# Combining the expert results of a two-layer block: accumulating transfers from GpSimd instead of loads and TensorE sums

## The chip, the cores and the metric

The kernel runs on one core of one Trainium2 chip. The metric is the device time of one execution in microseconds (us), the median of several runs. A core has TensorE (PE in the rows; PEld is its weight load), VectorE (DVE), ScalarE (ACT), GpSimd (POOL) and SyncE (SP), and 16 DMA engines that move data between the device memory and the on-chip memory. Each engine runs its own instructions in program order and waits on semaphores for the others.

## The reference

All arithmetic is float32. Two layers over 1040 rows (16 meta rows and 1024 tokens) of 1024 columns: layer 0 mixes by a state-space recurrence and differential attention, layer 1 by a gated linear recurrence (RG-LRU). After each mixer stands a layer norm and then a mixture of experts, each token going to two of 32 experts:

```
for i in range(DEPTH):
    mix = mixer_i(h)
    h = _layer_norm(ALPHA * h + mix, ln1_g, ln1_b)
    h = _layer_norm(ALPHA * h + _hier_moe(h, ...), ln2_g, ln2_b)
return h[:, N_META:]

def _layer_norm(z, g, b):
    mu = mean(z); var = mean((z - mu)**2)
    return (z - mu) * rsqrt(var + LN_EPS) * g + b
```

`_hier_moe` gives for a token the sum over its two experts of gate times expert output; ALPHA is the fourth root of 4, about 1.41. The change is in how the second of these two norms gets its input in each layer.

## The kernel before

**Stages.** The program is a chain of phases; a phase ends when all engines have met (`end_phase`). In order: layer 0's mixer, layer 0's experts and combining (`experts_and_combine`, layer 0), layer 1's mixer (`rglru_and_project`), layer 1's experts and combining. The rows are cut in 9 tiles (`TILES`): tile 0 with 16 meta rows, tiles 1 to 8 with 128 rows each. Layer 1 doesn't compute tile 0 in its combining, so it has 8.

**Experts.** SP loads the experts' weights in 96 units of 2 MB into a ring of 10 slots at the bottom of the on-chip memory (`l_w_ring`); each load waits until TensorE has read the unit that was in its slot. TensorE multiplies, ScalarE and VectorE scale each result by its gate (`K.gates`, `K.big_gate`), and GpSimd scatters the scaled rows with indirect DMAs to a buffer in device memory, `K.y_dram` (`expert_rows` in the rows). It has 2 x 1040 rows: first results, then second results. The last work items are two experts with a full block each (`big(4)`, `big(5)`) and a pair of small ones. `OverBlocks` handles blocks that the main plan has no room for.

**Combining** (`class Combining`, line 2146). When GpSimd has seen its last scatter land, it counts up `rows_done` (line 1839). SP waits for that and then loads, for each tile, two tiles of expert rows (`l_y`, line 2177) and the old rows out of `K.h1_dram` into `K.H` (line 2178), four tiles ahead. The gain and bias of the norm are loaded behind the second tile (`Norm.load`, line 1027). TensorE adds the two expert tiles by products with the identity into PSUM (`y_sum`, line 2234); VectorE makes ALPHA times old row plus that sum (line 2215, two instructions a tile; the first tile is done wholly by VectorE in lines 2210 and 2211). Then the norm of the tile: VectorE takes statistics (lines 1034 to 1036), subtracts the mean and multiplies by the gain (1041), ScalarE takes the root (1056), VectorE the reciprocal (1045), ScalarE scales (1060), GpSimd adds the bias (1068). For the last tile VectorE does the last two in one instruction (1050), after a wait for GpSimd's bias additions of all tiles before it. SP stores the tile (2184), to `K.h2_dram` in layer 0 and to the output in layer 1.

**Layer 0 alone.** TensorE turns each finished tile (`turn`, line 2243) and ScalarE copies it to `K.hT` (line 2260), which the next phase multiplies. ScalarE's program is one row of instructions: `norm.scalar(j)`, then the copies of tile j - 2. Between its stores SP also loads the first two blocks of RG-LRU weights (lines 2289 to 2292) and eight parameter vectors, by channel, with one element to a descriptor (lines 2297 and 2299). At its end SP waits for all stores (line 2199), and the phase ends.

**The next phase.** TensorE starts with the products of line 2343. VectorE first works out a table of parameters (lines 2437 to 2455) that it needs from line 2411 on.

## Time and profile before

| | us |
|---|---|
| median of 3 runs | 2360.14 (2353.16 to 2363.47) |
| the profiled execution, its own time | 2359.76 |
| its span in the trace | 2357.8 |
| layer 0, from the last scatter's issue to the first product of the next phase | 1180.3 to 1251.7 |
| layer 1, from the last scatter's issue to the last instruction | 2298.8 to 2354.8 |

All positions are us from the start of the span. A timeline line has start, duration, engine, line of the kernel, operation, output<-inputs, and in square brackets how long the engine sat idle before it and what ended that. SPq and POOLq are the queues of instructions that issue DMAs.

### The profile page before, as it was taken

The page shows a single profiled execution, that of the slowest core. Times are in us where ns is not written, and L with a number is a line of the kernel's source. Part 1 is how long each engine was busy: PE and PEld are TensorE (multiplying, and loading weights), DVE is VectorE, ACT ScalarE, POOL GpSimd, SP SyncE. Part 2 cuts the span into 40 slices and gives each one's busy share as a digit, 9 for nine tenths or more (in the row PEclk, how much of TensorE's full clock was granted, in tenths as well). Part 3 has the DMA queues.
Part 4 walks back from the last instruction along what each step waited for, and adds up shares of the span by engine and source line. Part 5 has one row for each costly group of instructions (what it writes and reads, how often), then busy time and mean ns, then how long its engine had stood idle before and what let it go on. Part 6 is the DMA issues. An engine that isn't in the chain of part 4 may idle for free. (4 is left out here: it accounts for less than half of the span.)

```text
span 2357.8 us, 33523 instructions
## 1 busy us (share of the span) xinstructions
PE 2188.0 (93%) x13475; PEld 1240.7 (53%) x13475; DVE 766.4 (33%) x1608; ACT 486.0 (21%) x904; POOL 308.5 (13%) x263
## 2 busy tenths in 40 slices
PE   7999999999689999999968999999967999999994
PEld 5787656655454555455434555555544455545541
DVE  7652236652611111111173444442261111111116
ACT  2222236611001001000023444431100100100001
POOL 7253000011011111111030000001101111111102
PEclk9999999999789999999988999999978999999998
DMA  4110002112399999899885111111239999989987
GB/s 159 38 37 1 21 1 72 32 40 70 141 401 418 420 419 418 343 398 410 368 298 165 40 32 29 40 39 37 71 135 395 414 421 418 420 350 393 413 367 306
DMA packets 148199, 529.81 MB, mean 225 GB/s; under 512 B 43874, under 2 KB 66946, under 8 KB 131664
## 3 DMA queue, kind: packets, MB, share of 16 engines
q1 hardware_dynamic: 134608, 493.84, 53.2%
q0 software_dynamic: 13312, 33.84, 3.7%
q8 instruction: 107, 1.75, 0.3%
q14 instruction: 44, 0.36, 0.0%
q10 hardware_dynamic: 128, 0.02, 0.0%
HBM read 499.99 MB, written 39.98 MB: 229 GB/s over the span
## 5 line engine op out<-in xcount | busy, mean ns | idle before, releaser
L1884 PE MATMUL l_main_pgu<-l_w_ring,l_ex_xT 128*64 128x256 f32 (+1 forms) x4992 | 473.5, 385 | 11.8 <-DMA l_w_ring<-in_l_moe_w_gate 8.5
L1884 PEld LDWEIGHTS l_main_pgu<-l_w_ring,l_ex_xT 128*64 128x64 f32 (+1 forms) x4992 | 285.6, 129 | 188.9 <-issue 41.5
L1930 PE MATMUL l_main_py<-l_w_ring,l_ex_hT 128*64 128x512 f32 (+1 forms) x1248 | 231.9, 595 | 1.9 <-DVE l_ex_hT L2002 1.9
L1881 PE MATMUL l_main_pgu<-l_w_ring,l_ex_xT 128*128 128x512 f32 x384 | 170.1, 597 | 1.7 <-DMA l_w_ring<-in_l_moe_w_gate 1.6
L1998 DVE TENSOR_TENSOR l_ex_hid<-l_ex_sil,l_main_pgu 128x256 f32<-128x256 f32 (+1 forms) x76 | 35.2, 463 | 376.0 <-PE l_main_pgu L1884 278.8
L2343 PE MATMUL lru_pr<-h2T,lru_wz 128*128 128x352 f32 (+1 forms) x480 | 144.4, 462 | 10.3 <-ACTq L2398 10.3
L2002 DVE COPY l_ex_hT<-l_main_ph 128x256 f32<-128x256 f32 (+1 forms) x76 | 35.4, 466 | 363.7 <-PE l_main_ph L1905 363.7
L2361 PE MATMUL lru_pg<-h2T,lru_wz 128*128 128x512 f32 x320 | 148.7, 592 | 0.0
L1930 PEld LDWEIGHTS l_main_py<-l_w_ring,l_ex_hT 128*64 128x64 f32 (+1 forms) x1248 | 69.2, 127 | 132.1 <-issue 124.8
L1976 ACT ACTIVATE l_ex_sil<-l_main_pgu 128x256 f32<-128x256 f32 (+1 forms) x76 | 31.7, 417 | 464.9 <-PE l_main_pgu L1884 372.5
L2343 PEld LDWEIGHTS lru_pr<-h2T,lru_wz 128*128 128x128 f32 x480 | 92.6, 193 | 63.1 <-ACTq L2398 10.7
L1881 PEld LDWEIGHTS l_main_pgu<-l_w_ring,l_ex_xT 128*128 128x128 f32 x384 | 71.2, 190 | 90.9 <-issue 87.0
L1822 POOL DMA_INDIRECT expert_rows<-l_ex_yb,half_row x64 | 64.2, 1003 | 414.4 <-issue 218.2
L308 PE MATMUL s_pa<-hT,w_in 128*128 128x260 f32 x512 | 114.7, 383 | 0.0
L1068 POOL TENSOR_TENSOR H<-H,l_ln_bias 128x1024 f32<-128x1024 f32 (+1 forms) x30 | 70.5, 2349 | 334.7 <-ACT H L1060 334.7
L1160 PE MATMUL lru_pr<-w_out,y1T 128*128 128x512 f32 x240 | 107.0, 602 | 0.0
L308 PEld LDWEIGHTS s_pa<-hT,w_in 128*128 128x128 f32 x512 | 96.9, 190 | 16.3 <-issue 1.7
L2361 PEld LDWEIGHTS lru_pg<-h2T,lru_wz 128*128 128x128 f32 x320 | 60.8, 190 | 57.1 <-issue 43.0
L1960 ACT COPY l_ex_xT<-l_main_px 128x512 f32<-128x512 f32 (+1 forms) x52 | 27.0, 520 | 295.0 <-PE l_main_px L1853 295.0
L2234 PE MATMUL l_main_pgu<-l_y,ident 128*128 128x512 f32 x88 | 45.2, 652 | 40.4 <-DMA H<-h_rows 40.1
L1041 DVE SCALAR_TENSOR_TENSOR H<-H,l_ln_mean_var,l_ln_gain 128x1024 f32<-128x1024 f32 (+1 forms) x34 | 50.5, 1485 | 95.5 <-PE lru_pg L1185 46.4
L1808 POOL DMA_INDIRECT l_ex_xb<-h_rows,x_idx x36 | 37.4, 1038 | 332.4 <-PE l_main_px L1853 212.3
...
## 6 DMA issues: line engine op xcount, KB each, us to landing
...
```

Of the source, the lines that this page charges most:

```text
L308: last = pe.matmul(pa[n % 2][:, 0:STEPS], w[:, k, P * (f % HEADS):P * (f % HEADS) + P], hT[:, k, j, :], start=k == 0, stop=k == KD - 1)
L1041: dve.scalar_tensor_tensor(out=z, in0=z, scalar=self.mv[0:m, 0:1], in1=self.gain[0:m, :], op0=ALU.subtract, op1=ALU.mult).then_inc(self.ga ...
L1068: pool.tensor_tensor(z, z, self.bias[0:m, :], ALU.add).then_inc(self.h_ready, 1)
L1160: last = pe.matmul(po[j % 2][h][0:m, :], self.slices[k][:, t0:t0 + m], self.w_out[:, k, 512 * h:512 * h + 512], start=k == 0, stop=k == ns ...
L1808: pool.indirect_dma_start(xb[xn % 2][0:m, :], None, K.h1_dram, bass.IndirectOffsetOnAxis(ap=index, axis=0), bounds_check=T - 1, oob_is_err ...
L1822: pool.indirect_dma_start(y_halves, bass.IndirectOffsetOnAxis(ap=K.half_row[:, it.column:it.column + 1], axis=0), yb[i % 2][:, 0:512], Non ...
L1881: last = pe.matmul(out[:], x[:, k, :], w[0][:, k, :], start=k == 0, stop=k == KD - 1)
L1884: last = pe.matmul(out[HALF * h + o:HALF * h + o + m, 0:256], x[:, k, it.at + o:it.at + o + m], w[n][:, k, 256 * h:256 * h + 256], start=k ...
L1930: last = pe.matmul(py[b][HALF * h + o:HALF * h + o + m, :], hT[:, c % 2, HALF * (c // 2) + o:HALF * (c // 2) + o + m], ws[n][:, c, 512 * h ...
L2234: last = pe.matmul(self.ps[j % 2][h][0:m, :], K.ident[0:m, 0:m], self.y[k][j % B][0:m, 512 * h:512 * h + 512], start=k == 0, stop=k == 1)
L2343: last = pe.matmul(pr[j][:, 0:c], wz[par][:, k, 0, :], K.hT[:, k, o:o + c], start=k == 0, stop=k == KD - 1)
L2361: last = pe.matmul(pgt[j][:, 0:c], wz[par][:, k, 1, :], K.hT[:, k, N_META + o:N_META + o + c], start=k == 0, stop=k == KD - 1)
```

## The change

It does five things.

- **Gates.** `K.gates` is scaled by 1/ALPHA, so that old row plus the two results is z/ALPHA; the norm gets LN_EPS/ALPHA² instead of LN_EPS and gives the same rows. The scaling takes the place of a copy.
- **Old rows ahead.** The tiles of `K.h1_dram` are loaded into a new buffer `z`, which lies in the ring's slots 6 to 8, as soon as the last units in these have been read, while the last experts are still being computed. Gain and bias follow when slot 9 has been read.
- **Accumulating transfers.** GpSimd adds both expert results onto `z` with DMAs that accumulate (`accum_op=ALU.add`), first results of tile j, and four tiles behind second results, each of which waits until the first one of its tile has landed. TensorE's sums and VectorE's additions are gone; VectorE's norm starts when both have landed and writes `K.H` from `z`.
- **RG-LRU loads.** The weights of the first two blocks are loaded when TensorE is done with the ring. The parameters are loaded as rows ahead of that, turned by one TensorE instruction at the start of the next phase, and copied by VectorE.
- **Stores.** Layer 0's stores are no longer waited for in their own phase, but in the next one ahead of `project.sync`.

The core of the diff:

```
+ROW_UNITS, NORM_UNIT = (6, 7, 8), 9
+LEAD = 4
@@ in route
-        do(dve.tensor_copy(K.gates[:], ptab[:, 1, :]))
+        do(ts(K.gates[:], ptab[:, 1, :], 1.0 / ALPHA, None, ALU.mult))
@@ experts_and_combine, SP, behind the last weight load
+            for unit in range(3 * NE):
+                if unit + UNITS >= 3 * NE and unit % UNITS in ROW_UNITS:
+                    unit_used(unit)
+            combine.load_rows(sp)
...
+            combine.load_norm(sp)
             sp.wait_ge(ya_ready, acts[N])
@@ GpSimd
             over.gpsimd(pool, blocks)
-            pool.sem_inc(rows_done, 1)
             combine.gpsimd(pool)
@@ TensorE
             over.tensor(pe)
+            pe.sem_inc(ring_free, 1)
             combine.tensor(pe)
@@ class Combining
+    def load_rows(self, sp):
+        for i in range(self.first, NT):
+            t0, m = TILES[i]
+            sp.dma_start(self.z[0:m, i, :], self.K.h1_dram[t0:t0 + m, :]).then_inc(self.rows_loaded, 16)
+
+    def load_norm(self, sp):
+        self.norm.load(sp, self.A[self.L + "_ln2_g"], self.A[self.L + "_ln2_b"])
+        if not self.last_layer:
+            self.K.lru.load_parameters(sp, self.free)
...
     def sync(self, sp):
+        if not self.last_layer:
+            sp.wait_ge(self.ring_free, 1)
+            K.lru.load_weights(sp, 0, 0)
+            K.lru.load_weights(sp, 1, 1)
+        for j in range(self.n):
             t0, m = TILES[self.first + j]
             sp.wait_ge(norm.h_ready, j + 1)
             sp.dma_start(out, K.H[0:m, self.first + j, :]).then_inc(self.stored, 16)
-        sp.wait_ge(self.stored, 16 * self.n)
+        if self.last_layer:
+            sp.wait_ge(self.stored, 16 * self.n)
 
     def gpsimd(self, pool):
+        def add(k, j):
+            t0, m = TILES[self.first + j]
+            if k == 1:
+                pool.wait_ge(self.added[j], 16)
+            pool.dma_start(self.z[0:m, self.first + j, :], K.y_dram[k * T + t0:k * T + t0 + m, :], accum_op=ALU.add).then_inc(self.added[j], 16)
+
+        pool.wait_ge(self.rows_loaded, 16 * n)
+        for j in range(n + LEAD):
+            if j < n:
+                add(0, j)
+            if j >= LEAD:
+                add(1, j - LEAD)
         for i in range(self.first, NT - 1):
             self.norm.gpsimd(pool, i)
 
+    def vector(self, dve):
+        do = Order(dve, self.order)
+        for j in range(self.n):
+            i = self.first + j
+            dve.wait_ge(self.added[j], 32)
+            self.norm.vector(dve, do, i, rows=self.z[0:TILES[i][1], i, :])
@@ rglru_and_project
         def _(sp):
+            sp.wait_ge(prm_turned, 1)
             load_w_out(sp, K, 1)
...
             sp.wait_ge(gate_ready, NG * NB)
+            sp.wait_ge(*K.h2_stored)
@@ TensorE
+            pe.wait_ge(R.loaded, 5 * 16)
+            pe.transpose(pa[0][:, 0:8 * NB], R.prm_rows[0:8 * NB, :], K.ident[0:8 * NB, 0:8 * NB]).then_inc(prm_turned, 1)
@@ VectorE
-            dve.wait_ge(R.loaded, 8 * 16)
+            dve.wait_ge(prm_turned, 1)
+            do(dve.tensor_copy(prm[:, 0:8, :].rearrange("p a n -> p (a n)"), pa[0][:, 0:8 * NB]))
```

`Combining.scalar` is not touched, nor is the body of `turn`.

Where GpSimd's program of layer 0 comes out of `OverBlocks` (the branches) and into the combining, before:

```order
L2046 UNCONDITIONAL_BRANCH
L2050 UNCONDITIONAL_BRANCH
L1068 TENSOR_TENSOR H<-H,l_ln_bias 16x1024
L1068 TENSOR_TENSOR H<-H,l_ln_bias 128x1024 x7
L1754 UNCONDITIONAL_BRANCH
```

and with the change (line 2218 is the accumulating DMA of `add`, 1069 the bias addition):

```order
L2061 UNCONDITIONAL_BRANCH
L2065 UNCONDITIONAL_BRANCH
L2218 DMA l_z<-expert_rows 16x1024
L2218 DMA l_z<-expert_rows 128x1024 x4
L2218 DMA l_z<-expert_rows 16x1024
L2218 DMA l_z<-expert_rows 128x1024 x12
L1069 TENSOR_TENSOR H<-H,l_ln_bias 16x1024
L1069 TENSOR_TENSOR H<-H,l_ln_bias 128x1024 x7
L1757 UNCONDITIONAL_BRANCH
```

Eighteen DMA issues now stand ahead of the first bias addition; before there was none.

SP's queue at the end of layer 0's combining, before, from the last tile's loads on:

```order
L2177 DMA l_y_5768<-expert_rows 128x1024
L2177 DMA l_y_5772<-expert_rows 128x1024
L2178 DMA H<-h_rows 128x1024
L2184 DMA h_rows<-H 128x1024
L2289 DMA lru_wz_5686<-in_l_w_in 128x8x128
L2290 DMA lru_wz_5686<-in_l_w_in 128x8x128
L2291 DMA lru_wax_5684<-in_l_lru_w_a 128x128
L2292 DMA lru_wax_5684<-in_l_lru_w_x 128x128
L2297 DMA lru_prm<-in_l_conv_w 128x10x1 x4
```

and with the change the same stretch, from the second block's weights to the end of the phase:

```order
L2289 DMA lru_wz_5687<-in_l_w_in 128x8x128
L2290 DMA lru_wz_5687<-in_l_w_in 128x8x128
L2291 DMA lru_wax_5685<-in_l_lru_w_a 128x128
L2292 DMA lru_wax_5685<-in_l_lru_w_x 128x128
L2207 DMA h_rows<-H 16x1024
L2207 DMA h_rows<-H 128x1024 x8
L1757 UNCONDITIONAL_BRANCH
```

Nothing but the waits for finished tiles now stands between SP's nine stores; before, both blocks of weights and the parameters stood between the fifth and the sixth.

ScalarE's program in layer 0's combining with the change (1057 the root, 1061 the scaling, 2259 the copies of a turned tile); its order is that of before:

```order
L1057 ACTIVATE l_ln_dev<-l_ln_var_eps 16x1
L1061 ACTIVATE H<-H,l_ln_rec_dev 16x1024
L1057 ACTIVATE l_ln_dev<-l_ln_var_eps 128x1
L1061 ACTIVATE H<-H,l_ln_rec_dev 128x1024
L1057 ACTIVATE l_ln_dev<-l_ln_var_eps 128x1
L1061 ACTIVATE H<-H,l_ln_rec_dev 128x1024
L2259 COPY h2T<-l_main_px 128x4x16 x2
L1057 ACTIVATE l_ln_dev<-l_ln_var_eps 128x1
L1061 ACTIVATE H<-H,l_ln_rec_dev 128x1024
```

Nothing moved here: the copies of tile 0 stand behind the scaling of tile 2 and ahead of the root of tile 3, as before.

## Rows read from the trace of the kernel before

**Rows 1.** Page, part 1: busy time, share of the span and instructions.

```profile
PE 2188.0 (93%) x13475; PEld 1240.7 (53%) x13475; DVE 766.4 (33%) x1608; ACT 486.0 (21%) x904; POOL 308.5 (13%) x263
```

**Rows 2.** Windows: length, engines' busy time (instructions), TensorE clock, DMA share, GB/s.

```profile
core 0: us, PE busy (x) PEld busy (x) DVE busy (x) ACT busy (x) POOL busy (x), PEclk, DMA share, GB/s
1130.00:1170.00 40.00, 39.03 (x221) 18.38 (x220) 4.35 (x7) 2.73 (x5) 1.95 (x2) 1.00 0.99 413
1170.00:1184.00 14.00, 7.57 (x43) 2.55 (x41) 1.83 (x3) 1.97 (x2) 1.96 (x2) 0.94 0.22 84
...
1190.00:1200.00 10.00, 5.84 (x8) 2.38 (x8) 4.44 (x8) 1.35 (x2) 0.23 (x1) 0.53 1.02 385
1200.00:1240.00 40.00, 34.23 (x124) 18.29 (x124) 37.97 (x64) 16.71 (x31) 18.60 (x8) 0.96 0.96 311
1240.00:1252.00 12.00, 1.70 (x8) 1.30 (x7) 0.37 (x4) 1.60 (x3) 0.00 (x0) 0.50 0.80 272
...
2291.00:2302.00 11.00, 5.09 (x37) 1.41 (x35) 1.83 (x3) 0.17 (x1) 1.97 (x2) 0.99 0.16 62
```

**Rows 3.** Timeline, layer 0: end of the experts, start of the combining.

```profile
1151.01 0.69 DVE L1998 TENSOR_TENSOR l_ex_hid<-l_ex_sil,l_main_pgu 128x512 f32<-128x512 f32 x1 [6.64 <-PE l_main_pgu L1881]
...
1180.29 0.98 POOL L1822 DMA_INDIRECT expert_rows<-l_ex_yb,half_row  x1 [3.87 <-DVE l_ex_yb L2010]
...
1184.49 1.37 SPq L2177 DMA_DIRECT2D l_y<-expert_rows  x2
...
1188.26 1.21 DVE L2210 SCALAR_TENSOR_TENSOR H<-H,l_y 16x1024 f32<-16x1024 f32 x1 [8.92 <-DMA H<-h_rows]
...
1196.71 1.27 DVE L1041 SCALAR_TENSOR_TENSOR H<-H,l_ln_mean_var,l_ln_gain 16x1024 f32<-16x1024 f32 x1 [4.20 <-DMA l_ln_bias<-in_l_ln_b]
```

**Rows 4.** Timeline, layer 0, VectorE and GpSimd: one tile of the steady part.

```profile
1213.76 1.28 DVE L2215 SCALAR_TENSOR_TENSOR H<-H,l_main_pgu 128x512 f32<-128x512 f32 x2
...
1215.12 2.37 POOL L1068 TENSOR_TENSOR H<-H,l_ln_bias 128x1024 f32<-128x1024 f32 x1 [2.48 <-ACT H L1060]
...
1216.72 1.85 DVE L1041 SCALAR_TENSOR_TENSOR H<-H,l_ln_mean_var,l_ln_gain 128x1024 f32<-128x1024 f32 x1
...
1218.60 0.69 DVE L2215 SCALAR_TENSOR_TENSOR H<-H,l_main_pgu 128x512 f32<-128x512 f32 x1
```

**Rows 5.** Timeline: end of layer 0's combining, start of the next phase.

```profile
1238.06 1.28 DVE L1050 SCALAR_TENSOR_TENSOR H<-H,l_ln_rec_dev,l_ln_bias 128x1024 f32<-128x1024 f32 x1
...
1239.40 1.97 PE L2243 MATMUL l_main_px<-ident,H 128*128 128x128 f32 x8 [0.57 <-DVE H L1050]
...
1241.17 3.48 SPq L2184 DMA_DIRECT2D h_rows<-H  x4
1241.40 1.07 ACT L2260 COPY h2T<-l_main_px 128x512 f32<-128x512 f32 x2 [1.47 <-PE l_main_px L2243]
...
1251.66 17.04 PE L2343 MATMUL lru_pr<-h2T,lru_wz 128*128 128x352 f32 x48 [10.30 <-ACTq L2398]
...
1269.21 0.82 DVE L2411 TENSOR_SCALAR lru_xc<-lru_rec,lru_pc 128x1040 f32<-128x1040 f32 x1 [9.81 <-ACT lru_rec L2378]
```

**Rows 6.** Timeline: a phase end with its stores not waited for, into layer 1's experts.

```profile
1735.33 0.26 DVE L1288 SCALAR_TENSOR_TENSOR logits<-lru_pa,l_ln_rec_dev,l_shift 128x36 f32<-128x36 f32 x1
...
1736.88 0.19 DVE L1611 TENSOR_REDUCE l_rt_cm<-logits 128x9 f32<-128x36 f32 x1 [1.30 <-PEq L2494]
```

**Rows 7.** Timeline, layer 1: last scatter, first load, last instruction.

```profile
2298.81 0.99 POOL L1822 DMA_INDIRECT expert_rows<-l_ex_yb,half_row  x1 [3.87 <-DVE l_ex_yb L2010]
2302.36 1.62 SPq L2177 DMA_DIRECT2D l_y<-expert_rows  x2
...
2353.49 1.28 DVE L1050 SCALAR_TENSOR_TENSOR H<-H,l_ln_rec_dev,l_ln_bias 128x1024 f32<-128x1024 f32 x1
```

**Rows 8.** Page, part 6: DMA issues, KB each, median us from issue to landing.

```profile
expert_rows<-l_ex_yb,half_row POOLq DMA_INDIRECT x64, 8.2
```

**Rows 9.** Line 1822 in 1150 to 1184: landing of layer 0's last scatter.

```profile
DMA to landing us min/median/max: 3.6/3.6/3.6
```

147 lines of the change are left out of this document (55 added, 92 removed).

## The prediction, made before the changed kernel ran

> **What bounds the kernel now.** I read the page first, then windows around the two places where the change works, then their timelines. TensorE is busy for 2188 of 2358 us [rows 1], and in the last 40 us of layer 0's experts for 39.0 of 40 [rows 2]: there the time is TensorE's, and nothing in the change touches its products. The combining is another matter. From 1200 to 1240 VectorE is busy for 37.97 of 40 us, TensorE for 34.2 (it adds expert rows there, which costs nothing while VectorE is later) and the DMA engines for 0.96 of the window at 311 GB/s [rows 2]. So VectorE sets the pace in that window, with the DMA engines close behind it: one tile every 4.84 us (line 2215 starts at 1213.76 and again at 1218.60) [rows 4].
>
> Two stretches are idle around it. The first tile's additions start at 1188.26, and VectorE then waits 4.20 us more for the norm's bias [rows 3]. At the end, ScalarE's last copy is done at 1241.40 + 1.07 = 1242.5, but SP issues the last four stores from 1241.17 to 1244.65, the phase waits for them to land, and the next phase's products start at 1251.66, 9.2 us after the copy [rows 5]. In layer 1 the combining starts at 2302.36 and VectorE's last instruction ends at 2353.49 + 1.28 = 2354.8 [rows 7].
>
> **Part 1: the end of layer 0's phase. Gain, 7.5 us.** The stores are waited for only in the next phase, ahead of work that is hundreds of us away. Another phase end in this trace has no such wait: last instruction ends at 1735.6, next phase's first starts at 1736.88, 1.3 us [rows 6]. So 9.2 shrinks to 1.3, less some 0.4 for the turn of the parameters, which now stands ahead of TensorE's products (one of eight products in a turn of 1.97 us takes 0.25) [rows 5]. VectorE's copy and parameter table are covered: it idles 9.81 us before line 2411 [rows 5]. If that cover were gone, a late parameter would cost its own lateness. The bounds are 6 and 8 us.
>
> **Part 2: old rows ahead. Cost: a later start of the adds, 3 us in layer 0, 2 in layer 1.** SP can load them when the up product of `big(5)` is read, just before 1151 [rows 3]; the weights in SP's queue before them keep the DMA engines full to about 1171 (share 0.99 up to 1170, then 0.22 over the next 14 us) [rows 2]. Nine tiles are 4.26 MB, 10.3 us at 413 GB/s; gain and bias 1.05 MB, 2.5 us; two scatters 1.9 us. That is 14.7 us behind 1171: 1185.7. It hides beside the last products, but the last scatter, issued at 1180.3, now travels in traffic. It took 3.6 us in silence [rows 9], the median over all is 8.2 [rows 8]; I take 3 of the 4.6 us between them, so GpSimd starts adding at 1184.3 + 3 = 1187.3. On top of that SP sends 2.36 MB of RG-LRU weights (5.7 us) from about 1180 on: the DMA engines are through with all that at 1191.4. In layer 1, with no RG-LRU loads, the weights end near 2291 (share 0.16 after it) [rows 2], and I put the start at 2302.1 + 2 = 2304.1.
>
> **Part 3: the price of an accumulating tile, u.** No row shows one, and the sum hangs on it. A plain tile of 0.524 MB takes 1.27 us at 413 GB/s and 1.36 at 385 [rows 2]: the lower bound, since the add can't move less. An add reads the expert rows and the old row and writes the sum: three passes where a plain load has two, 1.5 times, 1.9 to 2.0 us, if reads and writes cost alike; twice, 2.5 to 2.7 us, if the read side binds. I take the middle, **u = 2.3 us**, an estimate. For the issue on GpSimd the nearest row is the indirect DMA's 0.98 us [rows 3]; with some 0.3 for waits and registers, 1.3.
>
> The Trainium skill ("Collectives: The Full Stack", The bandwidth ceiling) says that a reducing transfer runs at half the rate of a copy because it needs two source reads, and gives a measured ratio of 1.93. By it u would be 2.45 to 2.6, a rival below; no row here shows it.
>
> **Part 4: layer 0's adds and norms.** GpSimd issues all 18 adds before its first bias addition. The last add waits for the first add of tile 8, which stands behind 11.1 tiles' worth of adds in the queue (a1 to a8, b1 to b3 and the small tile 0; a are first results, b second). The last issue is then at 1191.4 + 2.7 (landing and one issue) + 11.1u = 1194.1 + 25.5 = 1219.6. That matters for VectorE too, through ScalarE: ahead of the root of tile 3 stand the copies of tile 0, these wait for TensorE's turn, and this for GpSimd's bias addition of tile 0. So the norm stops at tile 3 until the adds are issued, although tiles 1 to 3 may have landed long before.
>
> From there: bias addition 2.4, turn 2.0, copy 1.1, root and reciprocal 0.3, 5.8 in all [rows 4, 5]. Then five more tiles on VectorE. Without the two line 2215 instructions (1.28, and gaps) a tile takes 4.84 - 1.32 = 3.52 [rows 4], so 17.6; and the last instruction 1.3: 24.7. The turn and copies at the end add 3.1, as before (1239.34 to 1242.5) [rows 5]. The copy ends at 1219.6 + 24.7 + 3.1 = 1247.4, 4.9 later than before. With part 1, layer 0 gains 7.5 - 4.9 = **2.6 us**. It also loses the 4.20 us bias wait and TensorE's adds, but both lie ahead of the stop and give nothing.
>
> **Part 5: layer 1.** No turns here, so ScalarE isn't held. The queue is a0 to a4, b0, a5, b1, a6, b2, a7, b3, b4 to b7. b3 lands at the start + 3.6 + 12u; from there tiles come faster (2.3 each) than VectorE takes them (3.52), and five tiles and the last instruction take 17.6 + 1.4. The end is 2304.1 + 22.6 + 27.6 = 2354.3, **0.5 us** sooner than 2354.8. GpSimd's bias additions don't bind: last issue at the start + 5 + 11u = 30.3, seven additions of 2.37 make 46.9, below 50.2. What follows the last instruction (one store) is as before.
>
> **The sum.** 2359.76 - 2.6 - 0.5 = 2356.7; the profiled run is 0.4 under the median, so no shift: **2357 us**. Each us on u costs 11.1 + 12 = 23.1 us over both layers. What a measurement of this kernel can tell from no change is about 0.5%, 11.8 us: u below 1.9 is faster by more, u above 2.9 slower. The gates' edit is an instruction for an instruction. The removed TensorE sums take the clock down earlier (it is 0.50 in the quiet windows [rows 2]), which I have paid for with 2.0 us a turn; before, the next phase started at 0.50 too.
>
> **Rivals.**
>
> *The adds run at the plain rate.* Then u = 1.3 and GpSimd's issue binds: 18 x 1.3 + 1 gives the last issue at 1187.3 + 24.4 = 1211.7, the copy at 1239.5, 3 sooner, 10.5 with part 1. Layer 1: b0 is the sixth issue and lands 11.4 after the start, eight tiles 28.2, last 1.4: 2345.1, 9.7 sooner. Sum 20: **2340 us**. For it: indirect transfers land in 3.6 us in silence, so the path itself is quick. Against it: an add moves half as much again. 0.2.
>
> *The read side binds,* so that an add takes about twice a plain tile, u = 2.55: 0.25 x 23.1 = 6 us more, **2363 us**, still within 0.5%. For it: in 1200 to 1240, with loads and stores mixed, the DMA engines were at 0.96 while moving 311 GB/s, less than with loads alone [rows 2]. 0.2. (This is what the rule of the Trainium skill, "Collectives: The Full Stack", The bandwidth ceiling, would make of it.)
>
> *Slower: an add goes through its passes one after another.* If reading old row, reading expert row and writing don't overlap within the DMA engines, u is about three plain tiles, 3.8, and the sum is 2356.7 + 1.5 x 23.1 = **2391 us**. Its place is the stretch up to the last issue in layer 0 and up to b3 in layer 1, and it decides from u = 2.9, or from an issue of 1.8 us on GpSimd if that binds instead (18 x 1.8 = 32 = 11.1 x 2.9). For it: nothing in this trace moves data so. [...] 0.22.
>
> *The forecast* without its neighbours: u between 1.55 and 2.9, 0.38, of which 0.13 lie under 1.9.
>
> **How the numbers follow.** Faster by over 0.5%: 0.2 + 0.13 = 0.33. Slower: 0.22. The rest, 0.45, is the forecast's main part and the second rival. The range takes in the plain rate at its end, 2340, and on the other side u = 3.2, 2357 + 0.9 x 23.1 = 2378. The unknown start (3 us in layer 0, 2 in layer 1, each may be 0 to 5) lies inside it.
>
> **What the profile after would show.** Accumulating DMAs on GpSimd's queue, GB/s in their window about 228 (0.524 MB in 2.3 us); VectorE idle in layer 0 from tile 2 to the end of the adds with ScalarE's wait for a turn behind it, then 3.5 us a tile; the next phase's products less than 2 us after the last copy; SP's row loads ending near 1182. Wrong would be the sum if the window of adds shows 390 GB/s or 130, if GpSimd's issues take well over 1.3 us, or if the last scatter lands much later than 1187.

## The result, and the profile after

The changed kernel takes **2381.07 us** (median of 6 runs, 2377.34 to 2383.67). The kernel before, run beside it, takes 2358.94 (2353.16 to 2363.47). The ratio is 1.010, 95% interval 1.0087 to 1.0112: slower by over 0.5%, and 3 us above the upper end of the range. The forecast was 2357.

The page of the changed kernel, busy time and the adds' row of the DMA issues (KB each, median us from issue to landing):

```profile
PE 2134.7 (90%) x13356; PEld 1220.8 (51%) x13356; DVE 757.9 (32%) x1575; ACT 486.3 (20%) x904; POOL 338.3 (14%) x297
...
l_z<-expert_rows POOLq DMA_DIRECT2D x32, 512.0 KB, 16.6
```

Against [rows 1], TensorE lost 53 us of work, VectorE 8.5, and GpSimd got 30 more, nearly all of it the issuing of 34 adds. No busy time says why the kernel is slower. Apart from the scaling of the gates and the loads that are sent ahead, all that changed lies behind the last scatter of each layer, so I measure everything from its issue:

| from the issue of the last scatter, us | before | after |
|---|---|---|
| layer 0: first load or add issued | 4.2 | 7.7 |
| layer 0: VectorE's last instruction ends | 59.1 | 77.0 |
| layer 0: next phase's products start | 71.4 | 83.2 |
| layer 1: first load or add issued | 3.6 | 8.6 |
| layer 1: VectorE's last instruction ends | 56.0 | 69.3 |

That is +11.8 in layer 0 and +13.4 in layer 1. The stretch from layer 0's next phase to layer 1's last scatter is 1047.15 us in both kernels. The span ends 4.3 us after VectorE's last instruction instead of 3.0, and this execution of the changed kernel came to layer 0's last scatter 3.5 us earlier (1176.81 against 1180.29). I don't count that as a gain: in the six runs built on the changed kernel or holding all that it loads ahead (the second, third, fifth, sixth, seventh and eighth below), the same scatter is issued anywhere from 1172.96 to 1182.77. Together 23.0, the difference of the two spans (2380.8 and 2357.8).

Timeline of the changed kernel, layer 0, GpSimd: last scatter, first and last adds, first bias additions:

```profile
1176.81 0.98 POOL L1837 DMA_INDIRECT expert_rows<-l_ex_yb,half_row  x1 [4.18 <-DVE l_ex_yb L2025]
1184.49 6.27 POOL L2218 DMA_DIRECT2D l_z<-expert_rows  x7 [6.69 <-issue]
...
1216.62 0.87 POOL L2218 DMA_DIRECT2D l_z<-expert_rows  x1 [4.71 <-DMA l_z<-expert_rows]
1222.16 0.87 POOL L2218 DMA_DIRECT2D l_z<-expert_rows  x1 [4.68 <-DMA l_z<-expert_rows]
1222.72 9.27 POOL L1069 TENSOR_TENSOR H<-H,l_ln_bias 16x1024 f32<-16x1024 f32 x4
```

The first add is 7.7 us behind the scatter (the first line answers to the scatter in [rows 3]). The last issues come one per 5.54 us, and each waits for the landing of an earlier add; an issue is paced by two adds, so an add takes 2.77. The bias additions start only behind the last issue, as forecast. The same stretches in windows, columns as in [rows 2]:

```profile
core 0: us, PE busy (x) PEld busy (x) DVE busy (x) ACT busy (x) POOL busy (x), PEclk, DMA share, GB/s
1188.00:1200.00 12.00, 0.00 (x0) 0.00 (x0) 0.00 (x0) 0.00 (x0) 6.72 (x9) 0.50 1.08 235
1200.00:1222.00 22.00, 0.00 (x0) 0.00 (x0) 11.38 (x23) 4.05 (x6) 4.79 (x6) 0.50 1.07 214
2334.00:2350.00 16.00, 0.00 (x0) 0.00 (x0) 9.63 (x20) 4.05 (x6) 4.85 (x5) 0.50 1.06 210
```

The DMA engines are full (1.06 to 1.08) while they move 210 to 235 GB/s; with plain loads and stores they moved 311 at 0.96 [rows 2]. Then the stop, and the tiles behind it, VectorE and GpSimd, layer 0:

```profile
1220.89 1.28 DVE L1042 SCALAR_TENSOR_TENSOR H<-l_z,l_ln_mean_var,l_ln_gain 128x1024 f32<-128x1024 f32 x1
...
1226.64 0.16 DVE L1046 RECIPROCAL l_ln_rec_dev<-l_ln_dev 128x1 f32<-128x1 f32 x1 [4.46 <-ACT l_ln_dev L1057]
1226.72 1.28 DVE L1035 BATCH_NORM_STATS2 l_ln_stats<-l_z 128x6 f32<-128x512 f32 x2
...
1228.35 4.73 DVE L1042 SCALAR_TENSOR_TENSOR H<-l_z,l_ln_mean_var,l_ln_gain 128x1024 f32<-128x1024 f32 x1
...
1234.47 2.34 POOL L1069 TENSOR_TENSOR H<-H,l_ln_bias 128x1024 f32<-128x1024 f32 x1 [2.48 <-ACT H L1061]
...
1234.75 3.15 DVE L1042 SCALAR_TENSOR_TENSOR H<-l_z,l_ln_mean_var,l_ln_gain 128x1024 f32<-128x1024 f32 x1
1237.82 0.15 DVE L1046 RECIPROCAL l_ln_rec_dev<-l_ln_dev 128x1 f32<-128x1 f32 x1
...
1239.29 2.34 POOL L1069 TENSOR_TENSOR H<-H,l_ln_bias 128x1024 f32<-128x1024 f32 x1 [2.47 <-ACT H L1061]
```

VectorE's reciprocal of tile 3 waits 4.46 us for ScalarE's root: the stop is there, at the tile that was named. But the tiles behind it take 1239.29 - 1234.47 = **4.82 us**, not 3.52. VectorE's subtract-and-multiply (line 1042, line 1041 before) takes 3.15 us; it took 1.85 in [rows 4] and 1.28 where GpSimd is quiet. It ends 1.09 us after GpSimd's addition ends (1236.81, 1237.90). Just behind the stop it takes 4.73 us and ends 1.09 us after the last of four queued additions (1231.99). The statistics of line 1035, which read one input from SBUF, take their usual 1.28 us in the middle of these additions (from 1226.72). The same in layer 1:

```profile
2307.12 0.98 POOL L1837 DMA_INDIRECT expert_rows<-l_ex_yb,half_row  x1 [3.87 <-DVE l_ex_yb L2025]
2315.76 4.50 POOL L2218 DMA_DIRECT2D l_z<-expert_rows  x5 [7.65 <-issue]
...
2347.42 7.25 POOL L1069 TENSOR_TENSOR H<-H,l_ln_bias 128x1024 f32<-128x1024 f32 x3
2349.11 1.29 DVE L1035 BATCH_NORM_STATS2 l_ln_stats<-l_z 128x6 f32<-128x512 f32 x2 [2.00 <-DMA l_z<-expert_rows]
...
2350.75 5.01 DVE L1042 SCALAR_TENSOR_TENSOR H<-l_z,l_ln_mean_var,l_ln_gain 128x1024 f32<-128x1024 f32 x1
...
2375.18 1.28 DVE L1051 SCALAR_TENSOR_TENSOR H<-H,l_ln_rec_dev,l_ln_bias 128x1024 f32<-128x1024 f32 x1
```

Three queued bias additions run back to back from 2347.42 to 2354.67, and VectorE's instruction, begun at 2350.75, ends 1.09 us after them. The end of layer 0, which answers to [rows 5]:

```profile
1252.52 1.28 DVE L1051 SCALAR_TENSOR_TENSOR H<-H,l_ln_rec_dev,l_ln_bias 128x1024 f32<-128x1024 f32 x1
...
1255.86 1.07 ACT L2259 COPY h2T<-l_main_px 128x512 f32<-128x512 f32 x2 [1.45 <-PE l_main_px L2245]
...
1259.44 0.37 PE L2372 MATMUL lru_pa<-ident,lru_prm_rows 80*128 80x80 f32 x1 [3.62 <-PEq L2500]
```

TensorE's turn of the parameters, its first instruction of the next phase, comes 2.5 us after the last copy (1256.93), and the products follow at 1259.97, 3.0 us after it instead of 9.2.

### The profile page after: what moved, and what is told of

Read it like the earlier page. It is cut to its first block and busy times, and to the rows that moved or that the text cites. A ratio compares the mean times of both kernels' runs of the same rounds, so it can differ in the third digit from the quotient of the medians.

```text
span 2380.8 us, 33236 instructions
## 1 busy us (share of the span) xinstructions
PE 2134.7 (90%) x13356; PEld 1220.8 (51%) x13356; DVE 757.9 (32%) x1575; ACT 486.3 (20%) x904; POOL 338.3 (14%) x297
## 5 line engine op out<-in xcount | busy, mean ns | idle before, releaser
L1944 PEld LDWEIGHTS l_main_py<-l_w_ring,l_ex_hT 128*64 128x64 f32 (+1 forms) x1248 | 69.3, 127 | 132.2 <-issue 124.7
L2364 PEld LDWEIGHTS lru_pg<-h2T,lru_wz 128*128 128x128 f32 x320 | 60.8, 190 | 57.1 <-issue 43.0
L1867 PE MATMUL l_main_px<-ident,l_ex_xb 128*128 128x128 f32 (+1 forms) x416 | 57.4, 281 | 21.3 <-DMA l_ex_xb<-h_rows,x_idx 21.3
```

The lines of the kernel that those rows point to most:

```text
L1867: last = pe.transpose(px[k // 4][:, k % 4, 0:m], xb[xn % 2][0:m, :].rearrange("s (p c) -> s c p", c=KD)[:, k, :], K.ident[0:m, 0:m])
L1944: last = pe.matmul(py[b][HALF * h + o:HALF * h + o + m, :], hT[:, c % 2, HALF * (c // 2) + o:HALF * (c // 2) + o + m], ws[n][:, c, 512 * h ...
L2364: last = pe.matmul(pgt[j][:, 0:c], wz[par][:, k, 1, :], K.hT[:, k, N_META + o:N_META + o + c], start=k == 0, stop=k == KD - 1)
```

## The experiments

The theory after this reading has three parts. **P**, the pace: while GpSimd adds the bias from SBUF, a VectorE instruction with both inputs in SBUF stands still; what was taken off VectorE was filled by that. **A**, the adds: an accumulating transfer takes twice the DMA engines' time of a plain one. **S**, the start: what is loaded ahead makes the last scatter land late. The rival, **V**, is the reasoning of the forecast: VectorE's busy time is the pace, the rest is noise. Ratios are to the kernel before, run beside each one on the same chip (2355.7 to 2356.5 us), with 95% intervals. The changed kernel's 2381.07 was measured beside 2358.94, so a plain difference between it and a run below holds up to 3 us that belong to neither. Distances from the last scatter for all kernels are in a table at the end of this section.

**Kernel before without VectorE's additions.**

```diff
-                dve.scalar_tensor_tensor(out=z[:, c], in0=z[:, c], scalar=ALPHA, in1=self.ps[j % 2][h][0:m, :], op0=ALU.mult, op1=ALU.add).then_inc(self.z_done, 1)
+                dve.sem_inc(self.z_done, 1)
```

> The kernel before, with VectorE's two additions a tile in the combining (line 2215, 1.3 us a tile) left out for every tile but the first; everything else runs, so the norm works on the old rows alone. Theory P (the pace is a ring: VectorE's reciprocal, ScalarE's scaling 1.15, GpSimd's bias addition 2.35, and only then the rest of VectorE's multiplication by the gain, since the two don't run side by side): a tile still takes 4.8 us, line 1041 grows from 1.85 to about 3.1 us, the total changes by less than 4 us. Rival V (VectorE's own work is the pace, as the prediction had it): 3.5 us a tile, 16 tiles, about 20 us faster, 2339.

Measured: 2356.14 us, ratio 1.0002 (0.9989 to 1.0015). Its timeline, VectorE and GpSimd:

```profile
1212.21 2.35 POOL L1068 TENSOR_TENSOR H<-H,l_ln_bias 128x1024 f32<-128x1024 f32 x1 [2.48 <-ACT H L1060]
...
1212.74 2.90 DVE L1041 SCALAR_TENSOR_TENSOR H<-H,l_ln_mean_var,l_ln_gain 128x1024 f32<-128x1024 f32 x1
...
1217.56 2.90 DVE L1041 SCALAR_TENSOR_TENSOR H<-H,l_ln_mean_var,l_ln_gain 128x1024 f32<-128x1024 f32 x1
```

1.3 us of work less on VectorE in each tile, and the tile still takes 4.82: the next instruction grew from 1.85 to 2.90, ending again 1.08 us behind GpSimd's (1214.56). V, which wanted 20 us, falls; P stands. It also says what VectorE's 37.97 busy us of 40 in [rows 2] were: in part time in which it was held.

**Changed kernel without GpSimd's bias additions** in the combining.

```diff
-        for i in range(self.first, NT - 1):
-            self.norm.gpsimd(pool, i)
+        for j in range(self.n - 1):
+            pool.wait_ge(self.norm.scaled, j + 1)
+            pool.sem_inc(self.norm.h_ready, 1)
```

> The changed kernel with GpSimd's bias additions of the combining left out (it only counts up the semaphore; the last tile keeps its bias). Theory P: line 1042 falls from 3.15 to 1.27 us and a tile on VectorE from 4.82 to about 2.95; five tiles behind the stop in layer 0 and five in layer 1 gain 1.9 each, the three that are queued up at the end of the adds some 5 more: 20 to 26 us, about 2358. Rival A (the accumulating transfers alone are to blame): the bias additions lie beside other work, at most 5 us faster, 2376.

Measured: 2358.35 us, ratio 1.0014 (1.0004 to 1.0023), 22.7 less than the changed kernel (19.5 when each is taken against its own kernel before). VectorE in layer 1:

```profile
2332.55 1.28 DVE L1042 SCALAR_TENSOR_TENSOR H<-l_z,l_ln_mean_var,l_ln_gain 128x1024 f32<-128x1024 f32 x1
...
2335.49 1.28 DVE L1042 SCALAR_TENSOR_TENSOR H<-l_z,l_ln_mean_var,l_ln_gain 128x1024 f32<-128x1024 f32 x1
```

The instruction is back at 1.28 us, a tile takes 2.94 where its data are there. So with GpSimd quiet a tile takes even less than the 3.52 of the forecast.

**Changed kernel, plain transfers in place of the accumulating ones.**

```diff
-            pool.dma_start(self.z[0:m, self.first + j, :], K.y_dram[k * T + t0:k * T + t0 + m, :], accum_op=ALU.add).then_inc(self.added[j], 16)
+            pool.dma_start(self.z[0:m, self.first + j, :], K.y_dram[k * T + t0:k * T + t0 + m, :]).then_inc(self.added[j], 16)
```

> The changed kernel with the same DMAs from GpSimd's queue as plain copies, without accumulating, so each tile ends up with the second expert's rows alone. Theory A (an add moves its bytes about twice): from 2.5 to 2.8 us a tile down to 1.3 or 1.4; layer 0's last issue comes 23 instead of 38 us after the first, layer 1's first tile 10 instead of 18 us after: 18 to 25 us faster, about 2360. Rival S (GpSimd's queue itself, its descriptors and waits, makes them slow): within 5 us of the changed kernel.

Measured: 2356.03 us, ratio 0.9999 (0.9983 to 1.0015), 25 less (21.8 against its own kernel before). GpSimd in layer 1:

```profile
2310.22 1.04 POOL L2218 DMA_DIRECT2D l_z<-expert_rows  x2 [0.24 <-DMA l_z<-expert_rows]
2311.50 1.04 POOL L2218 DMA_DIRECT2D l_z<-expert_rows  x2 [0.24 <-DMA l_z<-expert_rows]
```

Here a landing comes every 1.28 us and two issues follow each; later one issue comes per two landings, 2.56 us apart. So a plain tile costs **1.28 us** (DMA share 1.03 at 414 GB/s from 2308 to 2322), an accumulating one **2.5** (four arrivals in layer 1 from 2334.06 to 2349.11, two adds each, 2.51 an add). The ratio is 1.95. An issue costs GpSimd 0.53 us plain and 0.94 accumulating (medians of 34). A stands. The Trainium skill ("Collectives: The Full Stack", The bandwidth ceiling) gives a measured ratio of 1.93 between AllGather, which copies, and ReduceScatter, which adds. The 1.95 of these runs agrees; that a second read is the reason, as it says there, no run here shows.

Either cut alone gives back the whole loss, so the two don't add: with quick adds, the tiles queue at 4.8 us; with a quick norm, the adds are the end.

**Kernel before, with the stores waited for in the next phase**, the only part forecast as a gain.

```diff
-        sp.wait_ge(self.stored, 16 * self.n)
+        if self.last_layer:
+            sp.wait_ge(self.stored, 16 * self.n)
...
+            sp.wait_ge(*K.h2_stored)
             project.sync(sp)
```

> The kernel before with one part of the change alone: layer 0's stores are waited for in the next phase. SP still issues its last store at 1244.65, so the next phase starts 1.3 us later, at 1246 instead of 1251.7: 5.5 us faster, 2353. If the phase end waits for landing in some other way: no change.

Measured: 2348.21 us, ratio 0.9973 (0.996 to 0.9985), 7.6 less. In its trace the next phase's products start 3.9 us after the last copy instead of 9.2 (SP, ScalarE and TensorE):

```profile
1236.88 3.46 SPq L2187 DMA_DIRECT2D h_rows<-H  x4
1237.20 1.07 ACT L2264 COPY h2T<-l_main_px 128x512 f32<-128x512 f32 x2 [1.47 <-PE l_main_px L2247]
...
1242.20 1.54 PE L2348 MATMUL lru_pr<-h2T,lru_wz 128*128 128x352 f32 x2 [5.03 <-ACTq L2403]
```

The copy is done at 1238.27, but SP issues its last store until 1240.34, since weights and parameters stand ahead of its last four stores, as in the kernel before. From there it is 1.9 us to the products. In the changed kernel SP is through with its stores 2.8 us before the last copy ends.

**Changed kernel, RG-LRU weights later** (behind the fourth store instead of between the adds).

```diff
-        if not self.last_layer:
-            sp.wait_ge(self.ring_free, 1)
-            K.lru.load_weights(sp, 0, 0)
-            K.lru.load_weights(sp, 1, 1)
         for j in range(self.n):
...
+            if j == 3 and not self.last_layer:
+                sp.wait_ge(self.ring_free, 1)
+                K.lru.load_weights(sp, 0, 0)
+                K.lru.load_weights(sp, 1, 1)
```

> The changed kernel with one thing moved: the RG-LRU weights (2.36 MB), which SP issues in layer 0 as soon as the ring is free and which travel between the adds, are issued behind the store of the fourth tile instead. Nothing is left out. In layer 0 of the changed kernel two adds came through every 5.55 us, 2.77 us an add, in layer 1, without those weights, every 5.0 us, 2.5 an add. Theory 'the weights stretch the adds' expects layer 0's adds at 2.5 us as well: 11 add times before the last issue give 3 us, the weights' own 5.7 us are no longer in front of the adds, of which some part more comes back; the last issue of an add, at 1222.2 less the start of its phase, comes 4 to 6 us sooner, and the kernel takes 2375 to 2378 us. Rival 'the adds have a pace of their own in this layer' (old rows and sums of another layout, the turn's traffic) expects 2.77 us to stay and 2381 within 1 us.

Measured: 2375.3 us, ratio 1.0081 (1.0065 to 1.0098), within what was expected; its trace has layer 0 shorter by 4.2 us (79.0 instead of 83.2) and layer 1 as it was. Layer 0's arrivals come every 4.97 us, first to last issue takes 33.5 instead of 37.7 us:

```profile
1213.61 0.86 POOL L2218 DMA_DIRECT2D l_z<-expert_rows  x1 [4.11 <-DMA l_z<-expert_rows]
1218.58 0.86 POOL L2218 DMA_DIRECT2D l_z<-expert_rows  x1 [4.11 <-DMA l_z<-expert_rows]
```

So 2.5 us is the price of an add in both layers, and the 2.77 was the weights' share.

**Changed kernel, normalization finished on VectorE** for every tile, as it is for the last one.

```diff
-        if i == NT - 1:
+        if whole or i == NT - 1:
             dve.wait_ge(self.scales_ready, j + 1)
...
-        for i in range(self.first, NT - 1):
-            self.norm.gpsimd(pool, i)
```

> The changed kernel, with the combining's normalization finished on VectorE for every tile as it already is for the last one (one multiplication by the scale with the bias added, 1.28 us), so that neither GpSimd's bias addition (2.34 us) nor ScalarE's scale stands in it. Nothing is left out. Theory 'the ring VectorE, ScalarE, GpSimd, VectorE sets 4.8 us a tile, and the GpSimd addition stops VectorE's subtract-and-multiply' expects: that instruction back at 1.27 us instead of 3.15, tiles at some 4.4 us where they have all landed, no stop at tile 3 (ScalarE's copies no longer wait behind the adds in GpSimd's queue), so that the norm keeps up with the adds and ends some 6 us behind the last of them: layer 1's last instruction about 9 to 11 us sooner than in the changed kernel, layer 0's last copy 12 to 16 us sooner; 2355 to 2361 us in all. Rival 'VectorE's own work is the pace' (my forecast's reasoning: what counts is the busy time of VectorE) expects a tile to become longer by the 1.28 us, five tiles in each layer: 2381 + 2 x 6.4 less the stop, which is 2384 to 2394 us.

Measured: 2367.69 us, ratio 1.0056 (1.004 to 1.0073): 13 less than the changed kernel (10.9 against its own kernel before), with 15 bias additions more on VectorE, but 7 more than I expected. A tile takes 4.27 us, the subtract-and-multiply 1.28, and the stop at tile 3 is gone:

```profile
2342.59 1.28 DVE L1042 SCALAR_TENSOR_TENSOR H<-l_z,l_ln_mean_var,l_ln_gain 128x1024 f32<-128x1024 f32 x1
...
2346.86 1.28 DVE L1042 SCALAR_TENSOR_TENSOR H<-l_z,l_ln_mean_var,l_ln_gain 128x1024 f32<-128x1024 f32 x1
```

V's 2384 to 2394 is refuted once more. The end of layer 0's phase, ScalarE's last copy and TensorE's first instruction of the next:

```profile
1249.63 1.07 ACT L2257 COPY h2T<-l_main_px 128x512 f32<-128x512 f32 x2 [2.53 <-PE l_main_px L2243]
...
1252.11 0.37 PE L2370 MATMUL lru_pa<-ident,lru_prm_rows 80*128 80x80 f32 x1 [2.51 <-PEq L2498]
```

From copy to turn it is 1.4 us here, and 1.4 in all six runs below. The missed 7 us: I had the norm keep up with the adds, at 5.0 us a tile. But the last five tiles arrive 2.5 apart, and in layer 1 the fourth came 44.9 us after the scatter (42.0 in the changed kernel), its adds now travelling beside the stores of earlier tiles.

**All but the adds**: everything ahead as in the change, expert rows loaded plainly into four buffers, added by TensorE, and then by VectorE (line 2245) to the old rows.

```diff
+                dve.tensor_tensor(z[:, c], z[:, c], self.ps[j % 2][h][0:m, :], ALU.add).then_inc(self.z_done, 1)
...
-            dve.wait_ge(self.added[j], 32)
```

> All of the change but the accumulating adds: old rows, the norm's gain and bias and the turned RG-LRU parameters come ahead, and the stores are waited for in the next phase, but each tile's two expert rows are loaded plainly by SP into four buffers, added by TensorE into PSUM, and VectorE adds that to the old rows as before. RG-LRU weights are issued behind the fifth store. Nothing is left out. Theory 'the rest of the change is worth what it costs, the adds are the loss' expects the pitch of the kernel before, 4.8 us a tile in both layers (VectorE's subtract-and-multiply held to 3 us by GpSimd, or 1.85 with the two additions), no wait of 4.2 us for the bias, some 2 us less at the start against 3 more for the rows' traffic, and the 7.6 us of the stores: 2340 to 2350 us, against 2356 before. Rival 'the loading ahead costs in the experts' phase or at the start as much as it brings' expects 2352 or more.

Measured: 2358.76 us, ratio 1.001 (0.9997 to 1.0023). The rival's case: loading ahead costs as much as the stores bring. The tile takes 4.82 us as expected; what I missed is the start, 9.9 and 9.4 us behind the scatter. Two things make it up. The scatter lands after 7.0 and 6.1 us instead of 3.6 and 2.9, and SP then still waits for TensorE's word that the weight ring is free, which comes 11.7 us after TensorE's last product (why so late stays open; in the changed kernel SP's RG-LRU weights wait for the same word and start at 1186.02, 11.0 us after TensorE's last product). SP's waits from 1165 to 1200 (who waited for whom: us in total, times, longest):

```profile
SPq L2213 <- PEq L1967: 10.4, 1, 10.4
```

**Three products on TensorE**: it also adds the old rows, and VectorE reads the sum in PSUM.

```diff
-                terms = [self.y[0][j % B], self.y[1][j % B]]
+                terms = [self.z[:, first + j, :], self.y[0][j % B], self.y[1][j % B]]
```

> As the run before it, but TensorE adds three things in PSUM (old rows and both results), and VectorE takes its statistics and its subtract-and-multiply straight from PSUM in halves of 512 columns, with no addition of its own. Nothing is left out, the sums are made in another order. It tells apart what holds VectorE's subtract-and-multiply while GpSimd adds the bias (it took 1.27 us without that addition, 3.15 with it, both its inputs in SBUF). Theory 'both engines share a way into SBUF, and an instruction with one input from PSUM runs beside GpSimd' expects two halves of some 0.7 us each, unheld, and a tile at 3.6 to 3.9 us (TensorE's six products of 0.5 and its turn): 8 tiles in 2 layers at 1 us less than 4.84, 2325 to 2335 us. Rival 'VectorE is held whatever its input' expects 4.8 us a tile and what the run before it takes, 2340 to 2350 us.

Measured: 2371.59 us, ratio 1.0061 (1.0042 to 1.008). A miss, and inconclusive for its question: TensorE became the pace. A product of this width in fp32 is two instructions in the trace, 0.86 us from pair to pair (2345.03, 2345.89), and six products make 5.15 us a tile, and VectorE's instruction never fell together with GpSimd's addition:

```profile
2345.03 1.02 PE L2275 MATMUL l_main_ph<-l_z,ident 128*128 128x512 f32 x2
2345.89 1.88 PE L2275 MATMUL l_main_ph<-l_y,ident 128*128 128x512 f32 x4
...
2350.18 1.02 PE L2275 MATMUL l_main_pgu<-l_z,ident 128*128 128x512 f32 x2
```

**Only the norm's parameters ahead, and only the old rows ahead.** Both are the run before the last (no adds, stores waited for late) without the wait for TensorE's word. In the first the old rows come with each tile, in the second gain, bias and RG-LRU parameters come behind the second tile.

```diff
-        sp.wait_ge(self.ring_free, 1)
...
+            sp.dma_start(self.z[0:m, self.first + j, :], K.h1_dram[t0:t0 + m, :]).then_inc(self.loaded[j % B], 16)
```

> Which of the things loaded ahead makes the last scatter late? Before, it took 3.6 and 2.9 us to land, and the tile loads began 4.2 and 3.6 us after its issue; in the run with everything ahead and plain loads it took 7.0 and 6.1 us to land, and the loads began 9.9 and 9.4 us after it. Here only the norm's gain and bias (1.05 MB) and the RG-LRU parameters are loaded in the experts' last products; the old rows come with each tile's expert rows, as before. Nothing is left out; the stores are waited for in the next phase, and SP waits only for GpSimd's word that the rows are done. Theory 'it is the amount queued: 4.2 MB of old rows still on their way' expects 3.5 to 4 us to land, the loads to begin 4 to 5 us after the scatter's issue, no wait for the bias (7.4 us in both layers before): 2348 of the run with the stores alone, less 5 to 7, 2341 to 2344 us. Rival 'it is the two broadcasts, one row read 128 times, 13 to 15 us from issue to landing' expects 6 us or more to land, the loads 7 us after the scatter, and 2346 us or more.

> The counterpart: only the old rows are loaded in the experts' last products; gain, bias and RG-LRU parameters come behind the second tile's expert rows, about where the kernel before has them. Nothing is left out; stores and SP's wait as in the run before it. Theory 'the amount queued' expects the last scatter to land after 5 to 6 us, but since SP no longer waits for TensorE's word the loads to begin 6 to 7 us after its issue, the bias waited for as before or longer, and each tile to need a quarter less from the DMA engines: 2350 to 2355 us. Rival 'the two broadcasts' expects landing after 3 to 4 us, the loads 4 to 5 us after the issue, 2346 to 2350 us.

The old rows' loads ahead are gone in the first (`combine.load_rows` is not called); in the second the parameters' are:

```diff
-            combine.load_norm(sp)
...
+            if j == 1:
+                self.load_norm(sp)
```

Measured: 2350.79 us, ratio 0.9981 (0.9967 to 0.9995), and 2355.75, ratio 0.9998 (0.9986 to 1.0009). Last scatter of layer 1 and first tile loads, first kernel, then second:

```profile
2289.72 0.98 POOL L1833 DMA_INDIRECT expert_rows<-l_ex_yb,half_row  x1 [3.87 <-DVE l_ex_yb L2021]
...
2293.63 1.68 SPq L2201 DMA_DIRECT2D l_y<-expert_rows  x2
```

```profile
2295.72 0.99 POOL L1833 DMA_INDIRECT expert_rows<-l_ex_yb,half_row  x1 [3.87 <-DVE l_ex_yb L2021]
...
2302.55 2.04 SPq L2206 DMA_DIRECT2D l_y<-expert_rows  x4
```

3.9 us in the one, 6.8 in the other; in layer 0 4.7 and 7.6. So it is the old rows, 4.2 MB of them, and not the two broadcasts. That they act by their amount, still on its way, is the reading and wasn't tried with less. The first kernel did not reach its 2341 to 2344, though: the bias wait of 4.20 us [rows 3] is gone, but in layer 0 the second tile's statistics come 21.1 us after the scatter, against 20.9 before, and in layer 1 23.2 against 22.7. So that wait had not been what held the second tile.

**The sum written back into PSUM**, with the norm's parameters ahead: the same work, another place for one input.

```diff
-                dve.tensor_tensor(z[:, c], z[:, c], self.ps[j % 2][h][0:m, :], ALU.add).then_inc(self.z_done, 1)
+                dve.tensor_tensor(ps[h], z[:, c], ps[h], ALU.add).then_inc(self.z_summed, 1)
...
+                dve.scalar_tensor_tensor(out=out[:, c], in0=ps[h], scalar=N.mv[0:m, 0:1], in1=N.gain[0:m, c], op0=ALU.subtract, op1=ALU.mult).then_inc(self.z_done, 1)
```

> As the run with only the norm's parameters ahead, and one thing more: VectorE writes the sum of old rows and both results back into PSUM instead of SBUF and takes the statistics and the subtract-and-multiply from there, in halves of 512 columns. The same work, only the place of one input is changed; nothing is left out. It tells apart what the earlier run with three products on TensorE could not, since there TensorE was the pace at 5.15 us a tile and VectorE's instruction never ran beside GpSimd's addition. Theory 'VectorE is held only with both inputs in SBUF' expects halves of 0.70 us beside GpSimd's addition, not 1.85 for the two, so that a tile takes 4.84 - 0.5 = 4.3 to 4.4 us, eight tiles in two layers 7 to 8 us less where the DMA engines can keep up (they were at 0.96 to 1.0): 3 to 8 us below the run with the norm's parameters ahead. Rival 'held whatever its input' expects 4.8 to 4.9 us a tile and the same time within 1.5 us.

Measured: 2344.0 us, ratio 0.995 (0.9933 to 0.9967), 6.8 below the run with the parameters ahead. VectorE and GpSimd in layer 0:

```profile
1215.35 2.35 POOL L1069 TENSOR_TENSOR H<-H,l_ln_bias 128x1024 f32<-128x1024 f32 x1 [1.93 <-ACT H L1061]
...
1216.84 1.40 DVE L2247 SCALAR_TENSOR_TENSOR H<-l_main_pgu,l_ln_mean_var,l_ln_gain 128x512 f32<-128x512 f32 x2
...
1221.11 0.74 DVE L2247 SCALAR_TENSOR_TENSOR H<-l_main_pgu,l_ln_mean_var,l_ln_gain 128x512 f32<-128x512 f32 x1
```

VectorE's two halves take 1.40 us where GpSimd's addition (1215.35 to 1217.70) overlaps them, against 1.85 for the whole in [rows 4], and the half at 1221.11 lies wholly within the next addition and takes 0.74. All 34 halves of this run take 0.73 to 0.74 us, beside an addition or not. GpSimd's time is unchanged, and a tile takes 4.27. Halving came together with the move to PSUM; halves with both inputs in SBUF beside an addition were not run. P is now shown from three sides: VectorE's work taken away, GpSimd's taken away, one input moved. The Trainium skill states it ("SBUF — State Buffer", Who interferes with whom): a VectorE instruction with two inputs in SBUF contends with a GpSimd instruction that reads SBUF; one with at most one such input, outside the 2-port perf modes, does not. These runs agree (3.15 us against 1.28; 0.74 a half), and add that in fp32 the held instruction made next to no progress.

**The same, first tile added by VectorE from SBUF.**

```diff
+            if j == 0:
+                dve.wait_ge(self.loaded[0], 48)
+                do(dve.tensor_tensor(z, z, self.y[0][0][0:m, :], ALU.add))
+                dve.tensor_tensor(z, z, self.y[1][0][0:m, :], ALU.add).then_inc(self.z_summed, 2)
```

> A version put together from what the runs pointed to: stores waited for in the next phase, the norm's gain and bias ahead, old rows loaded with each tile, the sum written back into PSUM, and, new against the run before it, the first tile of each layer added by VectorE straight from SBUF as in the kernel before, so that TensorE, which runs at 1.2 GHz after the idle stretch, begins with the second tile. Nothing is left out. Theory 'the first tiles wait for TensorE at half clock' expects the first statistics 14 us instead of 18.3 us after the last scatter's issue in layer 1 and 10 to 11 instead of 16.3 in layer 0, the second tile's 2 to 4 us earlier in each, then 4.28 us a tile: 2344 less 4 to 7, 2337 to 2340 us. Rival 'the DMA engines bind there': the second tile's loads land no earlier, since they are behind the first tile's and at a share of 1.0, so that only TensorE's own time goes, under 1 us a layer: 2342 to 2344 us.

Measured: **2343.53 us**, ratio 0.9945 (0.9929 to 0.9961), 0.5 us below the run before it, which is within the spread. TensorE in layer 1:

```profile
2300.34 3.78 PE L2275 MATMUL l_main_pgu<-l_y,ident 128*128 128x512 f32 x4 [17.37 <-DMA l_z<-h_rows]
...
2303.91 2.52 PE L2275 MATMUL l_main_ph<-l_y,ident 128*128 128x512 f32 x4
...
2306.27 3.60 PE L2275 MATMUL l_main_pgu<-l_y,ident 128*128 128x512 f32 x8
```

It waits for the second tile's loads. The rival had the size: the first statistics come 4.1 us sooner in layer 1 and 5.2 in layer 0, and the second tile's only 0.2 and 0.4. But the loads are not all of it. TensorE, idle for 17.37 us before, has a granted clock of 0.50 (1.2 GHz) from 2300 to 2304 and of 1.00 (2.4 GHz) from 2306.4 to 2310, and the second tile's eight products take 6.1 us where the next eight take 3.6: the slow stretch has moved from the first tile to the second. What the loads alone cost, this run doesn't tell apart. This is the best version, faster than both kernels: the phase-end wait moved, the norm's parameters ahead, the sum in PSUM and the first tile on VectorE, without the adds and without the old rows ahead.

The distances from the last scatter's issue, us (layer 0: first issue, VectorE's last end, next phase's products; layer 1: first issue, VectorE's last end):

| kernel | L0 issue | L0 end | L0 next | L1 issue | L1 end | time |
|---|---|---|---|---|---|---|
| no VectorE additions | 4.7 | 58.7 | 71.3 | 3.8 | 55.0 | 2356.1 |
| after, no bias additions | 7.9 | 63.3 | 68.9 | 9.2 | 60.7 | 2358.4 |
| after, plain transfers | 7.8 | 62.8 | 68.8 | 8.2 | 57.0 | 2356.0 |
| stores only | 4.8 | 59.1 | 66.1 | 4.0 | 56.3 | 2348.2 |
| after, weights later | 7.9 | 73.0 | 79.0 | 8.8 | 69.5 | 2375.3 |
| after, norm on VectorE | 7.9 | 68.9 | 73.8 | 9.0 | 66.3 | 2367.7 |
| all but the adds | 9.9 | 66.0 | 70.9 | 9.4 | 60.5 | 2358.8 |
| three products | 9.9 | 75.7 | 79.7 | 9.2 | 62.9 | 2371.6 |
| parameters ahead | 4.7 | 59.4 | 64.3 | 3.9 | 57.1 | 2350.8 |
| old rows ahead | 7.6 | 62.4 | 67.3 | 6.8 | 57.1 | 2355.8 |
| sum back in PSUM | 4.8 | 56.9 | 61.8 | 3.9 | 52.9 | 2344.0 |
| first tile on VectorE | 4.5 | 56.5 | 61.1 | 3.9 | 52.9 | 2343.5 |

The two sums, L0 next and L1 end, explain the times: their change against before (71.4 and 56.0) plus 2356 gives each measured time within 3 us (the last row: -10.3 - 3.1, 2342.6; the changed kernel: +11.8 + 13.4, 2381.2).

## Why the prediction was wrong

By its own steps, where a term is the distance that it gave:

| step | forecast | measured | off |
|---|---|---|---|
| part 2, L0: scatter to first add | 7.0 | 7.7 | +0.7 |
| parts 3 and 4, L0: first to last issue | 32.3 | 37.7 | +5.4 |
| part 4, L0: last issue to VectorE's end | 24.7 | 31.6 | +6.9 |
| parts 1 and 4, L0: VectorE's end to next products | 4.8 | 6.2 | +1.4 |
| part 2, L1: scatter to first add | 5.3 | 8.6 | +3.3 |
| parts 3 and 5, L1: first add to b3 | 31.2 | 33.4 | +2.2 |
| part 5, L1: b3 to VectorE's end | 19.0 | 27.4 | +8.4 |
| last store | 3.0 | 4.3 | +1.3 |

Sum +29.6, less the 3.5 by which this execution was early: 26, and 2382.6 (the profiled execution's own time) is 26 above 2356.7.

No single line takes the sum out of its range: with the two lines to VectorE's end as forecast it would be near 2367, with nothing wrong but them near 2372.

- **The step that failed** is in parts 4 and 5: "Without the two line 2215 instructions (1.28, and gaps) a tile takes 4.84 - 1.32 = 3.52". It took 4.82. The two lines to VectorE's end are 15.3 of the 29.6 us. Of these, 10.6 are four tiles a layer at 4.82 and more instead of 3.52, and 6.0 the tile ahead of them, held until all queued bias additions were through (4.73 and 5.01 us for one instruction); the stop itself was 1.2 shorter than forecast. Subtracting a removed instruction from the pitch holds only if the others keep their length. The sign was there and wasn't read: line 1041 takes 1.85 us in [rows 4], where a GpSimd addition overlaps it by 0.77 us, and 1.27 in the same trace where GpSimd is quiet:

```profile
1202.79 1.27 DVE L1041 SCALAR_TENSOR_TENSOR H<-H,l_ln_mean_var,l_ln_gain 128x1024 f32<-128x1024 f32 x1
```

  What sets the pace now is a ring: reciprocal on VectorE, scale on ScalarE (1.15), bias on GpSimd (2.34), and VectorE's instruction, which can't end before that plus 1.1.
- **Part 3, the place right, the size low**: the DMA engines do pace the adds, but u was put at 2.3 and is 2.5 in layer 1 and, beside the RG-LRU weights, 2.77 in layer 0. That is 7.6 us. The second rival (2.55) had the size right, and by the slope of 23.1 it was worth 6; that the read side binds, its mechanism, no run shows. It was weighted 0.2 although the one figure that part 3 quotes spoke for it. The weights, for which part 2 had paid 4.1 us once, ahead of the adds, were in truth spread among them, and SP issued them from 1186.02 and not from about 1180, held by TensorE's word.
- **Part 2**: 3 and 2 us were taken for the late start, 3.5 and 5.1 came. In layer 1 I had let the weights end near 2291, and left out that old rows, gain and bias take some 12 us of the DMA engines behind them there too. Runs with rows alone and parameters alone put 2.8 to 2.9 us on the rows in each layer and nothing that can be measured on the parameters.
- **Part 1 was right**, mechanism and nearly size. In seven runs, the one with the norm on VectorE and the six behind it, TensorE's first instruction comes 1.4 us after the last copy and the products 1.8, against 1.7 forecast: a gain of 7.4 for 7.5. The run with the stores alone gains 5.3 by its trace (7.6 by the timed runs, whose interval holds 3.5 to 9.4), because SP is still issuing stores 2.1 us after the copy. In the changed kernel and three runs made from it the first instruction comes after 2.4 to 2.5 us and the products 0.4 to 0.5 later, a gain of 6.2 to 6.4. In these four GpSimd both issues the 18 transfers and has work or waits behind them; why that should cost 1.1 us stays open.
- **The stop at tile 3** (part 4) was right, place and mechanism, with 4.6 us from the last issue to the next tile instead of 5.8; the run that takes GpSimd and ScalarE's scale out of the norm has no stop.
- **The range**: the slower rival was put on u = 3.8 alone. None of the rivals let VectorE's gain vanish, though 15 us hung on it.
